# Residual products of 256 tokens with high and low activations side by side, and a later place for the output projections' first weight splits

## The reference, cut to what matters

```python
# D_MODEL 1024, 256 tokens (x) and 256 context tokens (ctx), DEPTH 2, D_FF 4096, D_FF_2 2816
def first_block(x, c, ctx, c_ctx, ...):
    for i in range(DEPTH):
        with_ctx = i < DEPTH - 1
        ...                                    # ada: silu(c) @ ada_w[i] + ada_b[i] in six parts, for x and for ctx
        ax = _modulate(hx, norm1_g[i], sx1, cx1)
        ac = _modulate(hc, norm1_g[i], sc1, cc1)
        if i % 2 == 0:
            yx, yc = _even_mixer(ax, ac, even_w_in[j], even_w_out[j], ...)   # window and neighbourhood heads
        else:
            yx, yc = _odd_mixer(ax, ac, odd_w_in[j], odd_w_out[j], ...)      # differential heads, x alone
        hx = hx + gx1 * yx
        hx = hx + gx2 * _mlp(_modulate(hx, norm2_g[i], sx2, cx2), mlp_w1[i], mlp_w2[i])
        if with_ctx:
            hc = hc + gc1 * yc
            hc = hc + gc2 * _mlp(_modulate(hc, norm2_g[i], sc2, cc2), mlp_w1[i], mlp_w2[i])
    return _rms_norm(hx, final_g)

def second_block(x, ...):
    for l in range(DEPTH):
        h = rmsnorm(x, attn_norm[l])
        ...                                    # w_in, mla_mixer (o_a) and dilated_attention (o_b)
        mixed = jnp.concatenate([o_a.reshape(B, S, -1), o_b.reshape(B, S, -1)], axis=-1)
        x = x + mixed @ w_out[l]
        x = x + conv_ffn(rmsnorm(x, ffn_norm[l]), w_up[l], conv_w[l], conv_b[l], w_down[l])
    return x
# kernel: second_block(first_block(...)); all inputs and the output are float32
```

## Time and profile before

| | us |
|---|---|
| median of three runs | 1782.37 (1782.04 to 1783.09) |
| profiled execution, its own time | 1783.51 |
| its span, first to last instruction | 1781.7 |
| TensorE busy (matmuls) | 1713.1, 96% of the span |
| VectorE busy | 1040.8, 58% |
| ScalarE busy | 833.8, 47% |
| mean granted clock of TensorE | 0.994 |

### The profile page before, as it was taken

How to read it: one execution, slowest core, us unless ns; L and a number is a source line. 1 busy time by engine, 2 the same in 40 slices (tenths; PEclk the granted TensorE clock), 3 DMA queues, 4 the chain that set the end, 5 groups by cost and what they waited for, 6 DMA issues and landing times.

```text
span 1781.7 us, 31653 instructions
## 1 busy us (share of the span) xinstructions
PE 1713.1 (96%) x12498; PEld 1513.6 (85%) x12498; DVE 1040.8 (58%) x1972; ACT 833.8 (47%) x1546; POOL 81.6 (5%) x90
## 2 busy tenths in 40 slices
PE   4999999999999999999899999999999999999998
PEld 2995567888888879985899999969999999699998
DVE  4426644634343445248565556675868657668675
ACT  3327754523232333236454445574645546755453
POOL 2100001000000022110000001000000000000000
PEclk8999999999999999999999999999999999999999
DMA  8817762433333334338356664613666536046663
GB/s 249 219 48 239 243 191 83 122 107 91 99 95 97 104 100 126 95 115 243 93 144 181 177 187 129 172 48 95 189 180 189 153 114 189 25 141 176 182 190 95
DMA packets 406258, 254.53 MB, mean 143 GB/s; under 512 B 8448, under 2 KB 405024, under 8 KB 406112
## 3 DMA queue, kind: packets, MB, share of 16 engines
q1 hardware_dynamic: 404576, 248.80, 47.9%
q0 software_dynamic: 1536, 3.71, 0.9%
HBM read 251.36 MB, written 1.11 MB: 142 GB/s over the span
## 4 chain that ended last, share of the span: by engine, by line
PE 87%; DVE 7%; ACT 3%; issue 2%; DMA 1%; SPq 0%; DVEq 0%; ACTq 0%
PE bank L2156 71%; PE bank L2407 3%; PE bank L2418 2%; PE bank L2314 2%; PE bank L2428 2%; PE bank L2135 2%; DVE parts L1123 1%; PE bank L2173 1%; DMA H<-ctx_t 1%; PE bank L2402 1%; PE bank L2434 1%; ACT parts L1306 1%; PE bank L2443 1%; ACT PR L1498 1%; PE bank L2351 1%
## 5 line engine op out<-in xcount | busy, mean ns | idle before, releaser
L2156 PE MATMUL bank<-AT,parts 128*128 128x256 f32 (+1 forms) x4704 | 675.1, 305 | 6.9 <-DVE parts L1123 2.9
L2156 PEld LDWEIGHTS bank<-AT,parts 128*128 128x128 f32 x4704 | 630.4, 190 | 49.7 <-issue 9.6
L1306 ACT ACTIVATE parts<-raw 128x1024 fp32r<-128x1024 f32 (+1 forms) x368 | 368.7, 1041 | 326.0 <-PE bank L2156 315.3
L1123 DVE TENSOR_TENSOR parts<-raw,parts 128x1024 fp32r<-128x1024 f32 (+1 forms) x368 | 434.6, 1212 | 145.0 <-ACT parts L1306 144.7
L2156 PE MATMUL bank<-HID,parts 128*128 128x256 f32 (+1 forms) x2592 | 397.3, 315 | 3.0 <-DVE HID L1805 3.0
L2156 PEld LDWEIGHTS bank<-HID,parts 128*128 128x128 f32 x2592 | 364.2, 191 | 34.3 <-DVE HID L1805 3.7
L2156 PE MATMUL bank<-parts,AT 128*128 128x256 f32 x2112 | 260.5, 285 | 3.8 <-DVE WORK L1948 1.8
L2156 PEld LDWEIGHTS bank<-parts,AT 128*128 128x128 f32 x2112 | 256.7, 193 | 6.3 <-DVE WORK L1948 2.3
L2036 DVE SCALAR_TENSOR_TENSOR H<-bank,MOD,H 128x256 f32<-128x256 f32 x120 | 52.6, 480 | 157.1 <-PE bank L2156 157.1
L1306 ACT ACTIVATE TOK<-bank 128x512 f32<-128x512 f32 (+2 forms) x160 | 71.2, 488 | 141.3 <-PE bank L2156 115.7
L2021 DVE TENSOR_TENSOR PR<-PR 128x512 f32<-128x512 f32 x48 | 33.2, 691 | 112.5 <-ACT PR L1550 112.5
...
## 6 DMA issues: line engine op xcount, KB each, us to landing
raw<-mlp_w SPq DMA_DIRECT2D x128, 512.0 KB, 4.2
...
raw<-even_w_in SPq DMA_DIRECT2D x12, 512.0 KB, 10.5
```

The lines of the kernel that those rows point to most:

```text
L1123: ng.tensor_tensor(chunk_part(c, 1), chunk_raw(c), chunk_part(c, 0).bitcast(F32), ALU.subtract)\
L1306: return nc.scalar.activation(o, i, ACT.Copy)
L2156: ins = MM(out, stay, move, start=opens and kt == 0 and i == 0, stop=kt == kts - 1 and i == 2 and stops)
```

## The change

Three edits belong together. Each narrow residual is now a unit for each output tile (t = 0, 1), as the wide ones were. Its product (`joined_product`) multiplies the high weights by high and low activations in one product of 512 columns, whose moving operand is two runs of 256 columns, into both halves of the bank, and the low weights by the high activations in one of 256 columns into the first half. VectorE adds first one half of the bank and then the other to the same tile of `H`, with a wait between the two. As a unit now reads one chunk of 128 columns, splits follow it one at a time. The statistic behind a narrow projection has one late tile instead of two.

A table `tails` moves the first four splits of `even_w_out` and `odd_w_out`. The fill-in transposes tied to their old places go by the rules above.

```diff
@@ project_out, mlp and the feed-forward of the second block
-            for t in ((0, 1) if wide else (None,)):
+            for t in (0, 1):
...
-                add("resid", ("resid", "ffn", l, n, None), layer=l, n=n, g=g, t=None, panel=pan, wide=False, src="HID",
-                    gate=None, kts=2 * pairs, group=("conv", l, g))
+                for t in (0, 1):
+                    add("resid", ("resid", "ffn", l, n, t), layer=l, n=n, g=g, t=t, panel=pan, wide=False, src="HID",
+                        gate=None, kts=2 * pairs, group=("conv", l, g))
@@ plan
-            if x.wide:
+            if x.wide or x.kind == "resid":
                 x.chunks = x.chunks[x.t:x.t + 1]
...
+    tails = {("even_w_out", 0): ("value", jobs[-8]["j"]), ("even_w_out", 1): ("flush", 0),
+             ("even_w_out", 2): ("resid", "even_w_out", 0, 0, 0), ("even_w_out", 3): ("resid", "even_w_out", 0, 0, 1),
+             ("odd_w_out", 0): ("mix", last_heads[-2]["j"]), ("odd_w_out", 1): ("mix", last_heads[-1]["j"]),
+             ("odd_w_out", 2): ("turn_o", 1, 2), ("odd_w_out", 3): ("turn_o", 1, 3)}
...
+        if (c.name, c.c0 // P) in tails:
+
+            at = max(at, units.index(index[tails[c.name, c.c0 // P]]))
@@ statistics: tiles summed late, squares taken early
-                    x.late_tiles = 1 if x.width == 2 * N else 2
+                    x.late_tiles = 1
...
-                    run = before[-8:] if units[before[-1]].wide else before[-4:]
+                    run = before[-8:]
@@ sync: output
-            last = [x for x in units if x.kind == "resid"][-4:]
-            for x in last:
+            last = [x for x in units if x.kind == "resid"][-8:]
+            for first_half, x in zip(last[::2], last[1::2]):
+                consumed(sp, first_half.u)
                 consumed(sp, x.u)
@@ vector: resid
-                    if x.gate is None:
-                        h = H[:, 2 * x.n:2 * x.n + 2, 0:N]
-                        V.tensor_tensor(h, b.rearrange("p (a t) -> p a t", a=2), h, ALU.add).then_inc(drained, 1)
...
+                    kt = 2 * x.n + x.t
+                    for v in range(2):
+
+                        h = H[:, kt, v * N:(v + 1) * N] if x.wide else H[:, kt, 0:N]
+                        if v and not x.wide:
+                            settle()
+                        if x.gate is None:
+                            ins = V.tensor_tensor(h, b[:, v * N:(v + 1) * N], h, ALU.add)
+                        else:
+                            g = v if x.wide else 0
                             ins = V.scalar_tensor_tensor(h, b[:, v * N:(v + 1) * N],
...
@@ tensor
+            def joined_product(out, x, tiles, other, ready):
+
+                for kt in tiles:
+                    ready(kt)
+                    wh, wl = (of_chunk(x, lambda c, part=part: chunk_part(c, part), kt, x.t * P, P) for part in range(2))
+                    both = ((out[:, :, :], wh, other(kt)), (out[:, 0, :], wl, other(kt)[:, 0, :]))
+                    for i, (to, stay, move) in enumerate(both if kt == 0 else both[::-1]):
+                        ins = MM(to, stay, move, start=kt == 0 and i == 0, stop=kt == x.kts - 1 and i == 1)
+                return ins
...
-                        for tiles in ([range(6), range(6, KT)] if early == 1 else [range(kts)]):
-                            if early == 1 and tiles[0] or early == 2 and c == 1:
+                        for tiles in ([range(6), range(6, KT)] if early else [range(kts)]):
+                            if tiles[0]:
...
+                            if k == "resid" and not x.wide:
+                                last = joined_product(b.rearrange("p (a t) -> p a t", a=2), x, tiles,
+                                                      lambda kt: act_in[:, :, kt, lo:lo + w], lambda kt: hidden_wait(x, kt, x.t))
+                                continue
```

24 lines of the change are left out of this document (9 added, 15 removed).

## The result

The changed kernel took 1770.99 us in the median of four runs (1769.16 to 1772.27), the kernel before 1782.20 beside it. The ratio is 0.9932 [0.9920, 0.9945]: 11 us faster, where 23.2 was forecast, and outside the range given (1755.5 to 1769). The profiled execution took 1772.27, with a span of 1770.5.

The account below looks back on a forecast made before the run. TensorE was taken as the bound. Terms of -10.5, +0.2, -5.2, -5.0 and -2.7 sum to -23.2 us: 1783.51 profiled becomes 1760.3, and 1759.2 as the median; range for 8 in 10, 1755.5 to 1769.

Parts of the forecast that it names:

- Part 1, the joined product: Narrow residuals and output projections: 800 triples each lose one instruction of 13.3 ns, 359.7 to 346.6 ns; 10.6 us saved.
- rival A: Joined products: most of the instruction's 13.3 ns stays, only 2.5 goes; 2.0 us saved instead of 10.6, 1767.8; chance 0.14.
- Part 2, VectorE's cover: Narrow residuals: VectorE's two dependent updates a tile hide behind TensorE, costing nothing except +0.2 us at the very end.
- six k tiles of the next product: Beside a prepared norm: 4.3 us of products needing nothing of VectorE would cover its lag of some 1.1 us.
- Part 3, the odd burst: Odd attention's end: moving four splits out of one step saves 6.4 us, 0.35 and 0.8 come back; -5.2 us.
- the forecast wait: First odd output product: TensorE waits about 0.8 us anew for the fourth pair, delayed by a moved split.
- Part 4, the even burst: Even attention's end: values start 5.1 us sooner and run 0.9 faster, a split costs 1.05 back; -5.0 us.
- the values' return to full clock: Even attention's end: the value product, 2.82 us at a clock of 0.65, takes 1.95 at full clock; -0.9 us.
- Rival C: Either attention's end: the clock falls where fill-in transposes went, some 3 us run at the lower level; 1762; chance 0.08.
- Rival B: Attention ends: moved splits delay the mixes, so both ends together give 2 us instead of 10.2; 1767.4; chance 0.12.
- Part 5, the narrow norms: Three norms behind output projections: one late tile saves 0.6 us, a vanished TensorE wait 0.35; -2.7 us in all.
- Rival E: Residual stages: VectorE becomes the bound if a dependent update costs over 0.77 us; slower, 1817 at 1.05; chance 0.02.

Follow-up runs that it names:

- `wide_low`: Changed kernel with the low weights' product also made 512 columns wide, over high and low activations; one run, 1848.48 us.
- `prep_places`: Changed kernel with six weight splits put back behind the preparation and statistics units of the prepared norms, where they stood before; 1767.35 us, ratio 0.9911.
- `pool2`: Changed kernel with most of GpSimd's additions of the prepared norms' squares given to TensorE, all splits left in place; 1771.05 us, ratio 0.9931.
- `no_tails`: Changed kernel with the table `tails` empty, so the output projections' first splits stand where the planner puts them; 1779.13 us, ratio 0.9981.

## Why the prediction was wrong

**Part 1, the joined product: mechanism right, size 8.2 instead of 10.6.** The 13.3 ns an instruction is real (`wide_low` gives 226.9 for the joined form), and rival A falls: a triple went from 359.7 to 349.5, not to 357. What the sum did not have is the 2.9 ns a pair that a mixture of widths costs. It added the pace of two stretches that had one width each; no row of before had a mixture.

**Part 2, VectorE's cover: the step that failed.** The durations were right to the hundredth (a gated pair 1.00, an ungated one 0.88), and it named the place and its price without cover, 1.1 us, but put it at nothing. Against the same groups before, less 10.2 ns a pair, the price was 3.7 us in the MLP, 1.5 of them the clock that fell behind the waits, and 2.1 in the feed forward. It failed twice. It took the order of VectorE's and ScalarE's work at a prepared norm from before, though the half residuals deal the splits out otherwise; and it took the low parts at 0.87 wherever they stand. Moved beside GpSimd's additions they take 1.97 to 2.80. `prep_places` undoes the first and `pool2` the second, and each alone brings the last MLP group back to 26.1 us. That the clock would fall here no part of the forecast had.
That six k tiles of the next product "need nothing of it" was wrong too: after four it waits 0.82 and then 0.80 for L1858.

**Part 3, the odd burst: right, term by term** (1.06 from scores to transposes, 0.35 ahead of the last transposes). -6.02 at the start of the output products against -6.05, and then the forecast wait, 0.51 for 0.8.

**Part 4, the even burst: right in the profiled execution** (-4.74 against -5.0, clock 1.00), and there partly by luck. Its bound, the clock that falls in the longer pause, is what ten of fourteen executions show, at about 1.5 us. And of its gain 0.9 was the values' return to full clock, which hangs on the execution as well: `no_tails`, with the old places, also has them in 1.95. Rival C is part of the time, at half of the price given. Rival B falls with both parts.

**Part 5, the narrow norms: -0.9 each forecast, some -0.3 to -0.4 measured.** A second-block stage shortened by 0.96 and 1.08, of which the pairs are 0.65. The step that failed is "the split of ScalarE is done beside the last product": it starts at 1219.94, with that product's end, and the square stands behind it as before; the tile's dependent updates would have held it nearly as long. And the sums that left the tail (1.13 to 0.70) stand in front of the last four k tiles instead (1.46 to 1.89): TensorE has to do them there too, where it waits for nothing. Only the wait of 0.35 went.

**The rest.** 1.5 us is the opening, which lay between 54.7 and 57.6 us over the kernels here, none of which changes it, and 0.8 lies in the two attentions of the second blocks. Rival E, a bound VectorE, was the right mechanism in the wrong place: not in every panel, only in the two groups where a norm is prepared, and for a cause that it did not name.

In figures, of the 12 us between forecast and profile: prepared norms 5.8 (1.5 of it the clock), mixing of widths 2.3, narrow norms 1.9 less the pairs' share in them, so 1.3, opening 1.5, attentions 1.1. That makes the 12.
